# Expert weights loaded by need, one large expert moved, and a last stage whose loads follow the gathers

## The reference, cut to what matters

```python
expert_idx = g_sel[:, None] * EXPERTS_PER_GROUP + top_i          # two experts of 32 per token
y_rows = (silu(xb @ e_gate[e]) * (xb @ e_up[e])) @ e_down[e]     # 1024 -> 256 -> 1024, all float32
moe = segment_sum(y_rows * row_w, row_tok)
ple = einsum(p, w_pe) * sigmoid(einsum(h1, w_pg))
out = layer_norm(DN_ALPHA * h1 + moe + ple, ln2_g, ln2_b)
```

## Time and profile before

| | us |
|---|---|
| median of 3 runs | 2478.69 |
| lowest and highest run | 2473.69, 2479.65 |
| the profiled execution, its own time | 2473.88 |
| its span in the trace | 2472.2 |
| PE busy in the span | 2248.4 (91%) |
| DVE busy | 1158.0 (47%) |
| ACT busy | 729.2 (29%) |
| POOL busy | 335.9 (14%) |
| expert stage of layer 0, of layer 1 (first L2322 to last L2342) | 873.91 to 1190.14, 2076.45 to 2391.54 |
| last stage (first L2919 to the end of the span) | 2400.28 to 2472.2 |

### The profile page before, as it was taken

One profiled execution on the slowest core, in us unless ns is written; L12 is line 12 of the kernel. 1 busy time (PEld: TensorE's weight loads), 2 busy tenths in 40 slices (PEclk: granted clock), 3 DMA queues, 4 the chain that ended last, 5 costly groups with the idle time before them and its releaser, 6 DMA issues. The chain is left out here.

```text
span 2472.2 us, 39715 instructions
## 1 busy us (share of the span) xinstructions
PE 2248.4 (91%) x14448; PEld 1161.8 (47%) x14448; DVE 1158.0 (47%) x2944; ACT 729.2 (29%) x1454; POOL 335.9 (14%) x514
## 2 busy tenths in 40 slices
PE   7999987988999999799599999688889999979977
PEld 3555554557455433233255555455655544323323
DVE  3444445665786222122345554466558652222226
ACT  2555553443211111000145555444423111100012
POOL 1021007830000200000000000296000020000011
PEclk9999998998999999899799999899999999999989
DMA  9476127732510969998653421565323156999956
GB/s 344 156 262 232 59 68 189 195 73 114 190 56 13 360 255 367 418 420 361 232 194 94 125 74 50 151 187 142 125 72 146 31 230 237 366 395 420 420 203 257
DMA packets 229645, 511.91 MB, mean 207 GB/s; under 512 B 60614, under 2 KB 138382, under 8 KB 204088
## 3 DMA queue, kind: packets, MB, share of 16 engines
q1 hardware_dynamic: 182760, 385.68, 43.2%
q0 software_dynamic: 27136, 85.62, 9.7%
q10 hardware_dynamic: 19552, 38.02, 4.1%
HBM read 382.90 MB, written 126.32 MB: 206 GB/s over the span
## 5 line engine op out<-in xcount | busy, mean ns | idle before, releaser
L507 PE MATMUL pj_zp<-pj_w,pj_xT 128*128 128x512 f32 (+1 forms) x1280 | 504.6, 541 | 4.3 <-DMA pj_w<-in_w_in 3.5
L507 PEld LDWEIGHTS pj_zp<-pj_w,pj_xT 128*128 128x128 f32 x1280 | 225.3, 192 | 203.0 <-issue 193.9
L2322 PE MATMUL op_bank<-ex_wgu,h 128*32 128x512 f32 x2688 | 298.7, 596 | 4.1 <-DMA ex_wgu<-in_e_up 4.1
L2145 PE MATMUL op_bank<-op_wout,op_hT 128*128 128x512 f32 x512 | 227.1, 601 | 1.5 <-DVE op_hT L2611 1.5
L2859 DVE TENSOR_TENSOR ex_h<-ex_sil,op_bank 128x256 f32<-128x256 f32 x42 | 17.7, 421 | 369.6 <-ACT ex_sil L2508 369.6
L2342 PE MATMUL op_bank<-ex_wd,ex_hT 128*32 128x512 f32 x1344 | 157.7, 611 | 25.6 <-DMA ex_wd<-in_e_down 24.1
L2322 PEld LDWEIGHTS op_bank<-ex_wgu,h 128*32 128x32 f32 x2688 | 83.9, 110 | 193.6 <-issue 190.2
L2145 PEld LDWEIGHTS op_bank<-op_wout,op_hT 128*128 128x128 f32 x512 | 97.4, 193 | 119.2 <-issue 116.7
L2508 ACT ACTIVATE ex_sil<-op_bank 128x256 f32<-128x256 f32 x42 | 16.1, 384 | 446.1 <-PE op_bank L2322 446.1
L1248 ACT ACTIVATE at_p<-at_s,at_nmx 128x640 f32<-128x640 f32 (+7 forms) x128 | 94.8, 740 | 173.0 <-DVE at_nmx L1211 172.5
L1159 PE MATMUL at_tp<-ident,at_p 128*128 128x128 f32 x576 | 89.0, 282 | 34.9 <-DVE at_pT L1217 24.9
(11 more groups left out here) (481 smaller groups left out, 3445.1 us busy)
## 6 DMA issues: line engine op xcount, KB each, us to landing
ex_wgu<-in_e_gate SPq DMA_DIRECT2D x64, 1024.0 KB, 13.0
ex_wgu<-in_e_up SPq DMA_DIRECT2D x64, 1024.0 KB, 15.3
ex_wd<-in_e_down SPq DMA_DIRECT2D x64, 1024.0 KB, 14.6
h<-scratch_XR SPq DMA_DIRECT2D x42, 512.0 KB, 15.4
scratch_XR<-pj_zero POOLq DMA_DIRECT2D x38, 512.0 KB, 7.7
pj_w<-in_w_in SPq DMA_DIRECT2D x8, 2048.0 KB, 15.6
pc_ckv<-in_cache_ckv SPq DMA_DIRECT2D x200, 64.0 KB, 2.0
cv_cch<-scratch_Z POOLq DMA_DIRECT2D x48, 256.0 KB, 4.3
```

What stands on the lines that cost most here:

```text
L507: last = pe.matmul(zp[c % ZB][:, 0:cn], xT[:, t % 2, k, :], w[:, k, c0:c0 + cn], start=(k == 0), stop=(k == KC - 1), skip_group_check=True)
L2145: last = pe.matmul(op[n][:, :], hT[:, t, c, :], wout[:, c, n * 512:(n + 1) * 512], start=(c == 0), stop=(c == KC - 1))
L2322: last = pe.matmul(gu[q % 2][part], xT[q % 2][:, c, part], wgu[s][:, :, c, :], start=(c == 0), stop=(c == KC - 1), skip_group_check=True)
```

## The change

There are three edits.

1. In the sorted order, the turn with 4 units goes to position 12, and the expert that was there becomes the last turn, with 2 units. The routing has five more DVE instructions for it, three ahead of the table of turns and two behind.
2. SP's loads of the expert stage are sorted by the later of two keys: when the place is free, and when the load is needed less `LEAD` = 2 quads. The waits of each load are the same as before. Rows, gate/up and down of one key value are no longer grouped by kind.
3. In the last stage SP loads the base rows of tile 0, waits for the gathered rows of tile 0, loads g and b, then the base rows of tiles 1 and 2, and each further tile t after the gathered rows of tile t - 2. PE runs the base product of tile 0 before it waits for a diagonal, waits for the two diagonals of each tile, and runs the base product of tile t + 1 behind the gathered products of tile t.

```diff
-TURNS = [2] * TWOS + [3] * (TRIPLES - 1) + [4]
+TURNS = [2] * (TWOS - 1) + [4] + [3] * (TRIPLES - 1) + [2]
...
+LEAD = 2
...
-                    todo.append((last_quad(was) + 0.5 if was is not None else HALVES - 0.2, 0, load_gate_up, e))
-                    todo.append((last_quad(was) + 1.5 if was is not None else HALVES + 0.8, 1, load_down, e))
-                todo += [(q - XSLOTS - 0.5, 2, load_rows, q) for q in range(XSLOTS, QUADS)]
-                for _, kind, load, n in sorted(todo, key=lambda a: a[0:2]):
+                    free = last_quad(was) if was is not None else HALVES - 0.7
+                    todo.append((max(free + 0.5, first_quad(e) - LEAD), 0, load_gate_up, e))
+                    todo.append((max(free + 1.6, first_quad(e) + 1.35 - LEAD), 1, load_down, e))
+                todo += [(max(q - XSLOTS - 0.35, q - 0.6 - LEAD), 2, load_rows, q) for q in range(XSLOTS, QUADS)]
+                for _, kind, load, n in sorted(todo, key=lambda a: (a[0], a[3])):
...
+                do(TS(late[:, :], order[:, :], float(TWOS - 1), None, ALU.is_equal))
+                do(TT(late[:, :], late[:, :], ty[:, :], ALU.subtract))
+                do(dve.scalar_tensor_tensor(order[:, :], late[:, :], float(NE - TWOS), order[:, :], ALU.mult, ALU.add))
...
+                do(TS(tx[:, :], order[:, :], float(TWOS), float(2), ALU.is_ge, ALU.mult))
                 do(TS(late[:, :], order[:, :], float(TWOS), 0.0, ALU.subtract, ALU.max))
+                do(TT(late[:, :], late[:, :], tx[:, :], ALU.add))
...
-                for t in range(NT):
+                def load(t):
                     sp.dma_start(base[:, t, :], d["BASE"][rows(t)]).then_inc(loaded[t], 16)
-                    if t == 0:
-                        for buf, which in ((g, "ln2_g"), (b, "ln2_b")):
-                            sp.dma_start(buf[:, :], row_of_layer(d[which], layer)).then_inc(gains, 16)
+
+                load(0)
+                sp.wait_ge(gathered[0], 32)
+                for buf, which in ((g, "ln2_g"), (b, "ln2_b")):
+                    sp.dma_start(buf[:, :], row_of_layer(d[which], layer)).then_inc(gains, 16)
+                for t in range(1, NT):
+                    if t > 2:
+                        sp.wait_ge(gathered[t - 2], 32)
+                    load(t)
...
-                pe.wait_ge(diag_ready, 2 * NT)
-                for t in range(NT):
+                def bases(t):
...
+                def gathered_rows(t):
+                    pe.wait_ge(diag_ready, 2 * t + 2)
                     pe.wait_ge(gathered[t], 32)
...
+                bases(0)
+                for t in range(NT):
+                    gathered_rows(t)
+                    if t + 1 < NT:
+                        bases(t + 1)
```

## The result

| | us | ratio to before |
|---|---|---|
| before, median of 5 runs | 2477.22 (2473.69 to 2479.65) | |
| the change, median of 5 runs | 2460.47 (2458.93 to 2464.69) | 0.9942 [0.9928, 0.9956] |
| profiled execution before, own time and span | 2473.88, 2472.2 | |
| profiled execution of the change, own time and span | 2460.47, 2458.9 | |

The median of 2478.69 shown ahead is that of three of the five runs. The change is faster by 0.58%. A table of stages, read from PE's and SP's timelines of both, says where. "Start" is all that lies ahead of the first expert product, "middle" the stretch between the two expert stages (the end of layer 0 and the first half of layer 1), "last" the time from the first load of base rows to the end of the span (spans are given to 0.1 us, and so are these differences).

The account below looks back on a forecast made before the run. PE (busy 91%) and DMA were both taken as near their limit, with PE's waits for down loads the largest idle time. 2473.88 - 13.0 - 11.6 + 1.0 + 2.2 + 3.4 = 2455.9, plus 4.8 for the median: 2460.7 us, range 2451 to 2472.

Parts of the forecast that it names:

- Moving the large turn, layer 0: Layer 0 expert stage: 17.93 us of waits and slow products at quad 6 go, 4.95 come; net -13.0 us.
- the later wait: Gate/up load of turn 30 at quad 19: 0.5 us per layer taken, ends 0 and 4.1; +1.0 for both layers.
- Layer 1: Layer 1 expert stage: the 9.93 us wait and a slow product go, 1.56 joins the 1.96 wait; net -11.6 us.
- The reserve: Expert stage, quad 19: turn 30's gate/up load lands 10.5 us before need, while PE would arrive 13.0 earlier.
- The rival of 4.1 us per layer: Expert stages: no reserve, each layer pays 4.1 us of later waits instead of 0.5; 2467.9 us, chance 0.14.
- The third rival: Expert stages: DMA is the bound and takes nearly all back, waits spread over quads 9 to 19; 2477.3 us, chance 0.06.
- Five DVE instructions: Routing: PE waits for the chain's end, so it moves by 1.1 us per layer; +2.2 us for both.
- The last stage: Last stage: tile 0's gather lands sooner but tile 1's base rows later; +3.4 us, ends -5.2 and +7.0.
- Start and middle: Code outside expert and last stages: only the added routing instructions count, 1.1 us per layer, +2.2 us in sum.
- The advice that the prediction quoted: Last stage: issue a DMA early, compute, wait late; speaks against holding loads back, no price, same sign as +3.4 us.
- The first rival: Last stage gains: gathers alone are fast, SP gets over half the engines; -5.2 instead of +3.4 us, 2452.1 us, chance 0.14.

Follow-up runs that it names:

- change_again: The change without any edit, timed once more on another version's chip: 2460.62 us, ratio 0.9940 to the kernel before.
- down_before_gate: The change with the last stage of before, and turn 14's gate/up load moved behind turn 11's down load: 2457.91 us, ratio 0.9929.
- five_more_steps: The kernel before with loads ordered by need and five added routing instructions whose results are overwritten, no turn moved: 2471.30 us, ratio 0.9979.
- ranks_awaited: four_bases_early, with PE waiting for VectorE's last read of the two PSUM banks instead of the routing chain's end: 2443.51 us, ratio 0.9872.
- last_alone: The kernel before with only the new last stage, expert stages as before: 2479.81 us, ratio 1.0019.
- order_alone: The kernel before with only SP's expert loads ordered by need, large turn and last stage as before: 2464.40 us, ratio 0.9959.
- four_bases_early: The change with base rows of tiles 0 and 1 loaded before the gather's wait, 2 and 3 ahead of g and b, later loads one gather earlier: 2451.06 us.
- old_last: The change with the last stage of before (all base rows, g and b loaded first, one wait for all diagonals): 2459.35 us, ratio 0.9929.

## Why the prediction was right, point by point

The predicted median, 2460.7, and the measured one, 2460.47, agree more closely than the working did, and that closeness is luck. The sum took 18.0 us off the profiled execution, and it lost 13.4 (2473.88 to 2460.47). What made up for it is the reference: the forecast added 4.8 us for the profiled execution of before lying under the median, while the change's profiled execution is its own median. (With all five runs the median of before is only 3.3 above it.) As a ratio the forecast was 2455.9 / 2473.88 = 0.9927, just outside the measured interval. Term by term:

- **Moving the large turn, layer 0: right.** -12.5 with its 0.5 of later waits was expected, -11.1 measured. The wait for turn 11's down load was 2.90 (forecast 3.36) and its product was slow by 1.70 (1.59). The term that was small is the later wait: 2.22 us at quad 19, not 0.5. The place was the one named, the size the middle of the range of 0 to 4.1, and no slow product followed it.
- **Layer 1: right.** -11.1 was expected, -11.6 measured. The wait of 3.49 us is the 1.56 + 1.96 that the prediction joined. The product behind it ran in 3.64 us, not slowly, which gave back what the 1.70 at quad 19 took; change_again has the slow product there (5.34), so that part is chance.
- **The reserve.** The rival of 4.1 us per layer did not come; 2.22 and 1.70 lie halfway. The third rival's picture appeared only when the order was tightened further (down_before_gate), and cost nothing there.
- **Five DVE instructions: right in the wait.** 1.1 us per layer, in the change, in five_more_steps, and in ranks_awaited from the other side. What they cost in time beside it is the next but one point.
- **The last stage: right in sign, the size too small.** +3.4 was the forecast, +5.5 measured, with last_alone at +4.1 (76.0) as the other look. Three steps of the term were off. The gather landed faster (5.7, not 7.2), so g was issued 7.94 us behind the first load, not 9.4. But the base rows of tile 1 landed 13.0 us behind g's issue, not 10.7. In 2391 to 2394 POOL's queue, filled ahead, held 61% of the engines where the earlier trace rows had shown an even share: SP moved 0.44 MB in these 3 us and not 0.62, which as an estimate is 1 us of the 2.3. In the next 3 us it had its half, but at 0.55 MB, not 0.62, and that is some 0.4 us more; the rest is not assigned. And the slow products behind the wait cost 2.7 us ((3.78 + 4.07) against 5.15), not 1.6: the wait was 8.86 us and two groups of products followed it at the lower clock.
- **Start and middle: -1.8 and +5.9 against +2.2 forecast.** The forecast had the VectorE wait, 1.1 us in each, and nothing for the clock; 4.8 of the 5.9 is PE busy for longer with the same work. The same split over all profiles: the ten with the five instructions and the wait have a middle of 889.5 to 893.0 us (mean 891.2), the three without them 886.3, 886.9 and 888.8 (mean 887.3). Of the 3.8 between the means 3.1 is PE's busy time (799.7 against 796.6) and 0.7 its idle time. PE's busy time falls into two groups, 795.9 to 797.7 us (before, order_alone, last_alone and four of the ten) and 800.2 to 802.1 (the other six). One kernel has both: the change 800.9, change_again 797.2. So what lies beyond the wait is work at the lower granted clock. That all three without the five instructions are in the lower group may be chance or an effect of when PE then waits; no run separates the two.

The advice that the prediction quoted, from the Trainium skill ("DMA: Bandwidth & Descriptors", Rules for kernel authors), to issue early and wait late, has the sign of edit 3 right: with the order of before, all loads issued at once, the last stage is 72.5 us against 77.4. It is not borne out as a whole, since four_bases_early issues most of its loads later than before and has 66.3 against 71.9. The same page's fit for a GpSimd DMA (Anatomy of one DMA) gives 3.2 us for a gather, as an estimate; the trace has 5.73 us for it beside POOL's other gathers and one base load. The first rival had 4.1, so its larger gain from short gathers was not there. (By the working of the +3.4, with its 1.6 us of slow products, that estimate would make the stage 0.6 us shorter, not 2.2.)

## What to carry to other kernels

Here the large wait at the hand-over to new buffers was removed by changing what is needed there (a work item that takes a whole step alone), and only shortened by reordering the loads: alone the first shortened the two stages by 8.9 and 9.8 us, the second by 4.8 and 4.2, both by 10.6 each. When loads are held back to speed up a critical transfer, sort what is held back by the time of its need; the same idea made the last stage 4 to 5.5 us longer with the LayerNorm vectors in front, and 5.6 us shorter with four tiles' rows in front. And ask of each semaphore what its waiter really needs: here it was the last read of two banks, some 50 instructions ahead of the signal.

## What the runs showed of the hardware

The clock behind the 8.86 us wait, from stretches of the change's last stage (the third last number is the granted clock):

```profile
2393.00:2397.00 4.00, 0.63 (x2) 0.00 (x0) 1.38 (x5) 1.41 (x2) 3.09 (x4) 1.00 1.02 373
2399.00:2407.00 8.00, 4.51 (x6) 1.94 (x7) 0.00 (x0) 0.00 (x0) 5.11 (x6) 0.50 1.03 416
2407.00:2409.00 2.00, 2.00 (x6) 0.93 (x5) 0.34 (x1) 0.00 (x0) 0.00 (x0) 0.89 1.04 412
2410.00:2440.00 30.00, 30.00 (x71) 13.32 (x70) 25.06 (x48) 7.28 (x12) 0.00 (x0) 1.00 0.58 225
```

It fell to its lower level of 1.2 GHz during the wait and stayed there for some 5 us of work after 2402.49. What was not expected is how little the length of a wait says about it. Behind 2.90 us in layer 0 the product took 5.34 us, behind 3.49 in layer 1 it took 3.64. In layer 0 of old_last a longer wait left the product at full speed and a shorter one did not:

```profile
999.27 3.64 PE L2344 MATMUL op_bank<-ex_wd,ex_hT 128*32 128x512 f32 x32 [3.36 <-DMA ex_wd<-in_e_down]
...
1150.82 8.77 PE L2324 MATMUL op_bank<-ex_wgu,h 128*32 128x512 f32 x64 [1.78 <-DMA ex_wgu<-in_e_up]
```

And the same wait of 2.8 us for ACT was followed by 0 to 6 us at the lower level. The Trainium skill's page "TensorE: Matmul & The Clock Gate", Part 1, says of the start of a kernel that the number of its slow matmuls changes from run to run; the rows here show such a spread behind waits in the middle of a kernel too. A term for slow products is therefore best given as a range, not as one number: in these expert stages 0 to 1.7 us for a wait of 1.7 to 4 us, behind the wait for ACT 0 to 3.0.
